# Expert stage of a two-block transformer kernel: a third set of weight slots in turn use, and the token gather done with the token pieces standing in the array

## The reference, cut to what matters

```
t = h.reshape(512, 1024)
g_prob = softmax(t @ w_rg + b_rg)              # 4 groups, the best one is taken
e_prob = softmax(chosen group's 8 logits)      # the best 2 of its 8 experts
combine = ...                                  # weight of each token in each of 32 experts
for each expert:                               # w_gate, w_up: 1024 x 256; w_down: 256 x 1024
    hid = silu(t @ w_gate) * (t @ w_up) * combine
    y += hid @ w_down
```

## Time and profile before

| | us |
|---|---|
| median of 3 runs | 2391.44 |
| the profiled execution, whole time | 2384.57 |
| its span | 2382.7 |
| TensorE busy | 2136.4 |
| VectorE busy | 1111.9 |
| ScalarE busy | 710.4 |
| first gate product of pair 0 begins | 2071.80 |
| copy of the last pair's result by VectorE begins | 2338.56 |

### The profile page before, as it was taken

How to read it: one execution, slowest core, us unless ns; L and a number is a source line. 1 busy time by engine, 2 the same in 40 slices (tenths; PEclk the granted TensorE clock), 3 DMA queues, 4 the chain that set the end, 5 groups by cost and what they waited for, 6 DMA issues and landing times.

```text
span 2382.7 us, 41675 instructions
## 1 busy us (share of the span) xinstructions
PE 2136.4 (90%) x17976; PEld 1483.7 (62%) x17976; DVE 1111.9 (47%) x1995; ACT 710.4 (30%) x1090; POOL 219.1 (9%) x97
## 2 busy tenths in 40 slices
PE   7978787879989999888899999989899999799994
PEld 5364646364447889665678888857555677456653
DVE  4445353544766555245477773252355643511113
ACT  2322222221221222354343332251244622422221
POOL 0020202020000000000133444310000000000001
PEclk9999999999989999999999999989999999899997
DMA  8201010103547555102323322245120132579994
GB/s 257 83 10 54 4 54 4 54 4 119 159 150 232 189 168 178 36 1 83 94 71 91 102 88 97 84 87 135 32 79 19 56 104 93 214 288 404 402 413 164
DMA packets 216315, 295.27 MB, mean 124 GB/s; under 512 B 7640, under 2 KB 191872, under 8 KB 207968
## 3 DMA queue, kind: packets, MB, share of 16 engines
q1 hardware_dynamic: 210784, 274.85, 34.2%
q0 software_dynamic: 3072, 9.74, 2.0%
q10 hardware_dynamic: 2304, 8.39, 0.9%
HBM read 279.84 MB, written 13.11 MB: 123 GB/s over the span
## 4 chain that ended last, share of the span: by engine, by line
PE 77%; DVE 8%; DMA 6%; ACT 5%; issue 4%; SPq 1%; POOL 0%; POOLq 0%; DVEq 0%; ACTq 0%
PE ps L678 12%; PE ps L1150 10%; PE ps L991 8%; PE ps L779 6%; PE ps L959 6%; PE ps L1181 5%; PE ps L1361 4%; PE ps L1015 3%; DMA ring<-in_w_up 3%; PE ps L1045 2%; PE ps L872 2%; PE ps L1061 2%; PE ps L1334 2%; PE ps L1132 2%; PE ps L1208 2%
## 5 line engine op out<-in xcount | busy, mean ns | idle before, releaser
L678 PE MATMUL ps<-hT,ring 128*128 128x512 f32 (+1 forms) x480 | 212.2, 598 | 3.1 <-ACT hT L1433 2.4
L779 PE MATMUL ps<-arena 64*64 64x64 f32 x6144 | 136.6, 231 | 51.0 <-issue 28.0
L1925 POOL TENSOR_TENSOR w_low<-ring,w_high 128x2048 fp32r<-128x2048 f32 x22 | 102.0, 4635 | 817.1 <-ACT w_high L1677 817.1
L678 PEld LDWEIGHTS ps<-hT,ring 128*128 128x128 f32 (+1 forms) x480 | 89.6, 188 | 120.0 <-issue 117.8
L779 PEld LDWEIGHTS ps<-arena 64*64 64x64 f32 x6144 | 120.3, 142 | 65.3 <-issue 55.0
L1150 PE MATMUL ps<-h_high,w_low 128*128 128x512 f32 x352 | 140.2, 398 | 5.7 <-DVE h_low L2342 5.7
L1150 PE MATMUL ps<-h_low,w_high 128*128 128x512 f32 x352 | 140.7, 400 | 0.0
L1150 PE MATMUL ps<-h_high,w_high 128*128 128x512 f32 x352 | 140.0, 398 | 0.0
L2248 DVE CUSTOM_DVE_ANT_0 arena<-ps,arena 128x256 f32<-128x256 f32 (+3 forms) x160 | 67.1, 468 | 124.8 <-PE ps L1061 124.7
L1463 ACT ACTIVATE arena<-ps 128x512 f32<-128x512 f32 x104 | 61.1, 597 | 190.1 <-PE ps L779 190.1
L1361 PE MATMUL ps<-ring,arena 128*64 128x256 f32 x960 | 111.3, 380 | 2.8 <-DMA ring<-in_w_up 2.0
(11 more groups left out here) (405 smaller groups left out, 4374.8 us busy)
## 6 DMA issues: line engine op xcount, KB each, us to landing
ring<-in_w_in SPq DMA_DIRECT2D x54, 1024.0 KB, 5.4
arena<-in_w_ada SPq DMA_DIRECT2D x80, 512.0 KB, 4.1
arena<-in_w_down SPq DMA_DIRECT2D x32, 1024.0 KB, 9.2
ring<-in_w_gate SPq DMA_DIRECT2D x30, 1024.0 KB, 9.7
ring<-in_w_up SPq DMA_DIRECT2D x30, 1024.0 KB, 10.9
ring<-in_w_up SPq DMA_DIRECT2D x44, 512.0 KB, 4.7
ring<-in_w_down SPq DMA_DIRECT2D x8, 1024.0 KB, 5.0
y_scratch<-arena ACTq DMA_DIRECT2D x16, 512.0 KB, 7.6
```

The source lines that it names most:

```text
L678: mm = pe.matmul(dst, w[:, k, hf * P:hf * P + width], rhs(k), start=(start and k == 0), stop=(stop and k == kts - 1))
L779: mm = pe.matmul(ps[o, bank + s, c % 4 * C:c % 4 * C + C], tmp[s][l][r, cc], eye64[r] if x is eye64 else tmp[s][x][r, cc], start=(i == 0), ...
L1925: pool.tensor_tensor(W_LOW[:, slot_, :], ring[:, slot_, :], W_HIGH[:, j % 2, :].bitcast(F32), ALU.subtract).then_inc(w_low, 1)
```

## The change

In words: (1) the loads of odd pairs (3, 5, ... 15) go to `SECOND_W`, those of even pairs stay in `EXPERT_W`, so that twelve buffers take turns. The waits on `gu_done` and `down_made` follow: each load waits for the reader two pairs back. For odd pairs in the loop SyncE also waits for a new semaphore `step_begun`, which VectorE counts up at the start of each step of two pairs; VectorE for its part waits at a round's start until the last round's rows are mixed. (2) In the gather, the token pieces stand and `PICKS` moves: 64 matmuls of 128 columns for 16 of 512. Their result has the features on the partitions already, so the copy to `TOK`, the 8 transposes and their semaphores are gone, and ScalarE copies straight to `XE`. The first gather now waits for all eight pieces of `H2_LOW`, not for four.

```diff
-                sp.wait_ge(*((gu_done, 7), (gu_done, 8), (down_made, 4))[part])
+                sp.wait_ge(*((gu_done, 5), (gu_done, 6), (down_made, 3))[part])
                 for e in range(2):
-                    expert_load(EXPERT_W[2 * part + e], w, c_, bass.ds(6 + e, 1), expert_full[2 * part + e])
+                    expert_load(SECOND_W[2 * part + e], w, c_, bass.ds(6 + e, 1), second_full[2 * part + e])
...
-                for j in range(2):
+                for j, buffers, full_ in ((0, EXPERT_W, expert_full), (1, SECOND_W, second_full)):
                     pair = q * 2 + j
+                    if j:
+                        sp.wait_ge(step_begun, q + 1)
                     for part, w, c_ in PARTS:
-                        sp.wait_ge(*((gu_done, pair * 2 + 1), (gu_done, pair * 2 + 2), (down_made, pair + 1))[part])
+                        sp.wait_ge(*((gu_done, pair * 2 - 1), (gu_done, pair * 2), (down_made, pair))[part])
...
             def gather(value, par, hf):
                 pe.wait_ge(placed, value)
-                for tt in range(4):
-                    for i_, x_ in enumerate((H2_LOW, H2_HIGH)):
-                        mm = pe.matmul(ps[:, hf, :], PICKS[:, par, tt, :], x_[:, tt, hf * 512:hf * 512 + 512],
-                                       start=(tt == 0 and i_ == 0), stop=(tt == 3 and i_ == 1))
+                for k in range(4):
+                    for tt in range(4):
+                        for i_, x_ in enumerate((H2_LOW, H2_HIGH)):
+                            rows = x_[:, tt, :].rearrange("s (p k) -> s k p", k=KT)
+                            mm = pe.matmul(ps[:, hf, k * P:k * P + P], rows[:, 4 * hf + k, :], PICKS[:, par, tt, :],
+                                           start=(tt == 0 and i_ == 0), stop=(tt == 3 and i_ == 1))
                 mm.then_inc(gathered, 1)
-            def turn_tokens(value, hf):
-                pe.wait_ge(tok_copied, value)
-                for k in range(4):
-                    mm = pe.transpose(ps[:, TOK_BANK[hf], k * P:k * P + P], tok_rows[:, hf * 4 + k, :], ident)
-                mm.then_inc(tok_turned, 1)
+            pe.wait_ge(h2_low, 8)
             for hf in range(2):
-                pe.wait_ge(h2_low, 4 * hf + 4)
                 gather(2, 0, hf)
-            for hf in range(2):
-                turn_tokens(2, hf)
...
-                turn_tokens(pair * 2 + 4, 0)
-                turn_tokens(pair * 2 + 4, 1)
...
-            def copy_tokens(value, hf):
-                act.wait_ge(gathered, value)
-                act.activation(TOK[:, hf, :], ps[:, hf, :], ACT.Copy).then_inc(tok_copied, 1)
             def tokens(value, par, hf):
-                act.wait_ge(tok_turned, value)
-                act.activation(XE[:, par, 4 * hf:4 * hf + 4].rearrange("p k s -> p (k s)"), ps[:, TOK_BANK[hf], :],
+                act.wait_ge(gathered, value)
+                act.activation(XE[:, par, 4 * hf:4 * hf + 4].rearrange("p k s -> p (k s)"), ps[:, hf, :],
                                ACT.Copy).then_inc(xe_ready, 1)
```

More of the change, by code:

```diff
@@ L303, in build @@
         PICKS = rounded("picks", offset_of["arena"] + 10240 * 4, 2, 4, 2 * SLOTS)
-        TOK = area(36864, 2, 512)
-        TOK_BANK = (7, 0)
         XE = area(8192, 2, 8, 2 * SLOTS)
@@ L319, in build @@
         RK, RM = area(15520, 4, 32), area(15648, 4, 34)
-        NRD, SINK = area(15844, 4), area(15848, 12)
+        NRD, SINK = area(15844, 4), area(15848, 16)
         IDX = area(15796, 8).bitcast(mybir.dt.uint32)
@@ L379, in build @@
         h2_high, h2_low = sem("h2_high_made"), sem("h2_low_made")
-        tok_copied, tok_turned = sem("tokens_copied"), sem("tokens_turned")
         logits_copied, logits_turned = sem("logits_copied"), sem("logits_turned")
@@ L391, in build @@
         fetched = [sem(f"fetched{i}") for i in range(4)]
+        step_begun = sem("step_begun")
         mixed = [sem(f"mixed_{i}") for i in range(4)]
@@ L649, in _ @@
                 quad = sp.snap(q % 8, min_val=0, max_val=7)
-                for j in range(2):
+                for j, buffers, full_ in ((0, EXPERT_W, expert_full), (1, SECOND_W, second_full)):
                     pair = q * 2 + j
+                    if j:
+                        sp.wait_ge(step_begun, q + 1)
                     for part, w, c_ in PARTS:
-                        sp.wait_ge(*((gu_done, pair * 2 + 1), (gu_done, pair * 2 + 2), (down_made, pair + 1))[part])
+                        sp.wait_ge(*((gu_done, pair * 2 - 1), (gu_done, pair * 2), (down_made, pair))[part])
                         for e in range(2):
-                            expert_load(EXPERT_W[2 * part + e], w, c_, bass.ds(quad * 4 + (2 * j + e), 1), expert_full[2 * part + e])
+                            expert_load(buffers[2 * part + e], w, c_, bass.ds(quad * 4 + (2 * j + e), 1), full_[2 * part + e])
             outv = a["out"].rearrange("(k p) t -> p k t", p=P)
@@ L1331, in gather @@
                 pe.wait_ge(placed, value)
-                for tt in range(4):
-                    for i_, x_ in enumerate((H2_LOW, H2_HIGH)):
-                        mm = pe.matmul(ps[:, hf, :], PICKS[:, par, tt, :], x_[:, tt, hf * 512:hf * 512 + 512],
-                                       start=(tt == 0 and i_ == 0), stop=(tt == 3 and i_ == 1))
-                mm.then_inc(gathered, 1)
-            tok_rows = TOK.rearrange("s h c -> s (h c)").rearrange("s (p k) -> s k p", k=KT)
-            def turn_tokens(value, hf):
-                pe.wait_ge(tok_copied, value)
-                for k in range(4):
-                    mm = pe.transpose(ps[:, TOK_BANK[hf], k * P:k * P + P], tok_rows[:, hf * 4 + k, :], ident)
-                mm.then_inc(tok_turned, 1)
+                for k in range(4):
[4 more added lines that the diff above has]
+                                           start=(tt == 0 and i_ == 0), stop=(tt == 3 and i_ == 1))
+                mm.then_inc(gathered, 1)
+            pe.wait_ge(h2_low, 8)
             for hf in range(2):
-                pe.wait_ge(h2_low, 4 * hf + 4)
                 gather(2, 0, hf)
-            for hf in range(2):
-                turn_tokens(2, hf)
             def expert_pair(pair, j, weights, full_, loaded):
@@ L1388, in _ @@
             with pe.Fori(1, rounds * 8) as q:
-                for j in range(2):
-                    expert_pair(q * 2 + j, j, EXPERT_W, expert_full, q * 32 + j * 16)
+                expert_pair(q * 2, 0, EXPERT_W, expert_full, q * 16 + 16)
+                expert_pair(q * 2 + 1, 1, SECOND_W, second_full, q * 16 + 16)
             for tt in range(4):
-                pe.wait_ge(mixed[tt], rounds)
+                pe.wait_ge(mixed[tt], rounds + 1)
                 for k in range(KT):
@@ L1863, in _, with tokens @@
             ybuf = a["y_scratch"].rearrange("(e t) d -> t e d", t=2 * SLOTS)
-            def copy_tokens(value, hf):
+            def tokens(value, par, hf):
                 act.wait_ge(gathered, value)
-                act.activation(TOK[:, hf, :], ps[:, hf, :], ACT.Copy).then_inc(tok_copied, 1)
-            def tokens(value, par, hf):
-                act.wait_ge(tok_turned, value)
-                act.activation(XE[:, par, 4 * hf:4 * hf + 4].rearrange("p k s -> p (k s)"), ps[:, TOK_BANK[hf], :],
+                act.activation(XE[:, par, 4 * hf:4 * hf + 4].rearrange("p k s -> p (k s)"), ps[:, hf, :],
                                ACT.Copy).then_inc(xe_ready, 1)
-            copy_tokens(1, 0)
-            copy_tokens(2, 1)
             tokens(1, 0, 0)
@@ L1883, in _ @@
                         act.activation(SG, ps[:, 2, 0:256], ACT.Silu).then_inc(silu_m, 1)
-                        copy_tokens(pair * 2 + 3, 0)
-                        copy_tokens(pair * 2 + 4, 1)
                         tokens(pair * 2 + 3, 1 - j, 0)
@@ L1896, in _ @@
                 for tt in range(4):
-                    act.wait_ge(mixed[tt], r + 1)
+                    act.wait_ge(mixed[tt], r + 2)
             for k in range(KT):
@@ L2582, in _ @@
             ts(SINK[:, 8:9], ZERO, 1.0, None, ALU.add).then_inc(gu_done, 2)
+            for tt_ in range(4):
+                ts(SINK[:, 12 + tt_:13 + tt_], ZERO, 1.0, None, ALU.add).then_inc(mixed[tt_], 1)
             def place(col_, par, second):
@@ L2610, in _ @@
             with dve.Fori(0, rounds) as r:
+                dve.wait_ge(mixed[0], r + 1)
                 ts(RANK_IN, RANK2, 0.0, SLOTS - 1.0, ALU.max, ALU.min).then_inc(round_link, 1)
@@ L2614, in _ @@
                 tt(IDX, RANK_IN, ROW0, ALU.add).then_inc(indexed, 1)
+                dve.wait_ge(mixed[1], r + 1)
                 tt(WGT_IN, RANK_IN, RANK2, ALU.is_equal).then_inc(round_link, 1)
                 dve.wait_ge(round_link, r * 5 + 2)
+                dve.wait_ge(mixed[2], r + 1)
                 tt(WGT_IN, WGT_IN, WGT, ALU.mult).then_inc(round_link, 1)
+                dve.wait_ge(mixed[3], r + 1)
                 ts(RANK2, RANK2, -float(SLOTS), None, ALU.add).then_inc(round_link, 1)
```

(1 more changed line is left out.)

## The result

The changed kernel takes 2600.61 us (median of 4 runs, 2598.14 to 2603.56) against 2393.78 us: ratio 1.0868, 95% interval 1.084 to 1.0897. It is 207 us slower. The forecast was slower by some 37 us, 2428 in a range of 2411 to 2450. The direction was right, the loss is five and a half times the forecast one.

A forecast was written before the change was run, and what follows sets the result against it. TensorE's work (16.2 us a pair) bounds the stage, weight loads close behind. 16 x 2.56 = 41.0, less 7.3 of waits, plus 3.8 at the start: 37.5 us more, taken as 2428; own range 2415 to 2441, widened to 2411 to 2450.

The forecast's parts named there:

- What bounds the kernel; the twelve buffers: Expert stage: TensorE's own work sets 16.2 us a pair, weight loads 16.8 in waiting pairs; the buffers save at best 7.3 us.
- the waits would stay at 16.2 us a pair: Expert stage: were TensorE still at 16.2 us, weights would need 420 GB/s and the waits for them would remain.
- The gather: 0.114 us a matmul: Expert gather: 64 matmuls of 128 columns, 0.114 us apart (0.108 to 0.119), take 7.57 us for 3.89.
- So the step costs nothing: Gather's standing token pieces, 8 elements apart: the turn's eight loads with that step lie 0.111 us apart, so no extra time.
- +3.68 a pair: Loss in each pair's gather, 7.57 us for 3.89; with -1.12 from the turn it makes 2.56 more a pair.
- The row of the turn's loads: Profile row of the turn's eight loads, step of 8 elements: (0.97 - 0.19) / 7 = 0.111 us each, read as the load's price.
- The clock: Expert stage: TensorE's times per pair were summed at full clock, 1.00, that is 2.4 GHz.
- Rival 5: Clock falls in the gathers, matmuls from 0.114 to 0.21 us for those 7 us; kernel above 2527; 3 in 100.
- Rival 4: Gather: rounded type at 128 columns takes plain float32 time, 0.21 us a matmul, gather 13.7; kernel 2527; 6 in 100.
- The turn and the exposed copy: Between gather and down products: 1.81 us of turn and wait go, 0.69 returns through VectorE's uncovered copy; 1.12 gained.
- The loads at that pace: Weight loads at 18.75 us a pair need 363 GB/s, under 403 shown; all arrive in time, 7.3 us of waits go.
- The start: First gather begins at 2065.0, half clock for some 24 matmuls; first gate product 3.8 us later (3 to 5).

## Why the prediction was wrong, point by point

- *What bounds the kernel; the twelve buffers.* Mostly right. There were 7.3 us to be had: the buffers alone gave 7.3 in the stage, and 9.5 and 11.5 in the medians of the two comparisons. The sentence that the waits would stay at 16.2 us a pair was wrong (none was left at 418 GB/s); the sum didn't use it.
- *The gather: 0.114 us a matmul.* This step failed. It rests on the sentence "So the step costs nothing", read from the turn's loads. The turn's loads were transposes, and for an ordinary load the step costs 0.13 us. Measured: 0.24 us, of which 0.111 is the distance in a row, inside the forecast range of 0.108 to 0.119, and the rest is the step. The sum's term of +3.68 a pair was +11.67.
- *A sign that was passed over.* The row of the turn's loads had it: (0.97 - 0.19) / 7 uses a length of 0.19, and the transposes at line 1369, whose operand lies in a row, have loads of 138 ns. A step that changes the length of a record by 40% isn't free, only hidden. I read the distance and not the length. The rule on 16-byte lines of the Trainium skill ("Advanced Engine Details and Errata", Memory Cachelines) speaks against this change by itself, and the prediction left it out.
- *The clock.* The sum took full clock in the stage; this was the second thing missed. Rival 5 had the place, and its time, above 2527, holds the 2601 measured, but that is luck: in its mechanism the distance of the gather's matmuls follows the clock, and it doesn't (0.24 at both levels). With loads in a row the clock stays up in the stage. Its fall costs through the down products, about 1.9 x 16 = 30 us of the 207, and some 0.2 a pair in the transposes behind the gather. No rival had a slow load. Rival 4 (2527) is refuted by the run with standing columns in a row.
- *The turn and the exposed copy:* 1.81 us gone, 0.69 forecast to come back. At full clock it is 0.26 + 0.44 + 0.04 = 0.74; in the changed kernel 0.96 at half clock. Right.
- *The loads at that pace:* right, for the slower pace too. No pair waits, and the stage's DMA share is 0.53.
- *The start.* A second term failed. The later begin was 2.6 (forecast 2.5), but from there to the first gate product it took 7.0 more, not 1.3. The forecast had the clock back after some 24 of the 64 matmuls, because 24 transposes of the same shape had brought it back. It stayed at half through all 64. The step is the smaller part of the 7.0: without it the same stretch (2079.27 to 2093.87 in the run with standing columns in a row) is 14.6 us for 9.28, that is 5.3 more. Why the clock stayed down, no run here tells.
- *With the step taken away,* the pair is as forecast, 18.61 us for 18.75, and so is the whole, 2434 us for 2428, inside the range. That the stage is right to 0.1 us (300.1 for 300.0) is luck: the pairs are 2.2 us shorter in all, and the first gate products, begun at half clock, take 9.16 for 7.13. The 6 us over the forecast are the start, 7.9 (2.6 + 5.3) for 3.8, and ScalarE's reordering copies, which take 1.8 us longer from the first to the last.

## What to carry to other kernels

Turning operands round in a matmul turns round which of them is read how. Before a tile becomes the standing one, look at the distance of its columns in store. At full clock, 8 bytes cost next to nothing (0.118 us a matmul for 0.111), and 16 and more double it, to 0.23 and 0.24 us for 128 float32 columns. Here rearranged copies, made once (eight of 1.05 us for 0.60), took the price away. When a row is used as the price of an operation, compare its length as well as its distance to that of its neighbours, and make sure that it is the same form: a transpose is no stand-in for a load of an ordinary matmul. And two changes made at once should be timed apart: here the good one (0.9965) was buried under the bad one.

## What the runs showed of the hardware that I had not expected

- An ordinary load of 128 standing float32 or rounded columns at 2.4 GHz: 192 ns in a row, 196 at 8 bytes, 329 at 16, 337 at 32. At 1.2 GHz the one in a row is 333 ns (distance 0.213 us) and the one at 32 bytes still 337 (0.24).
- As a transpose the same read is nearly hidden: 193 ns for 138, and 1.16 us for 1.09 in eight.
- Moving columns 32 bytes apart: 512 of them in 0.43 us for 0.228.
- The granted clock falls to 1.2 GHz in each run of 64 rounded matmuls with slow loads, though TensorE's records leave no gap, and it doesn't in the same run in plain float32, 0.24 us apart too.
- Begun at 1.2 GHz, a run of 64 rounded matmuls of 128 columns stayed there for all of its 13.9 us (0.50), with loads in a row and no gap; the old gather, 16 rounded matmuls of 512 columns, had the clock back at 2068.2, 5.7 us after its start.
